# Two norms and a weight split inside the delta rule's last turn, with projection products behind it

## What is computed

```python
proj = _rmsnorm(x, mix_norm[i]) @ w_in[i]
q, k, v, z, beta_logit, alpha, hy_in = jnp.split(proj, IN_SPLITS, axis=-1)
o_dn = _deltanet_group(q, k, v, z, beta_logit, alpha, ...)   # 4 heads, both directions
o_hy = _hyena_group(hy_in, ...)                              # 512 channels
x = x + jnp.concatenate([o_dn, o_hy], axis=-1) @ w_out[i]
...
for o, gate in enumerate((x1, x2)):                          # in _hyena_group
    zz = gate * (_fft_conv(zz, kspec[:, o]) + skip[o] * zz)
return _rmsnorm(zz, norm_w).astype(u.dtype)
```

## Time and profile before

| what | us |
|---|---|
| median of 3 runs | 4145.75 |
| lowest, highest | 4143.84, 4146.04 |
| profiled execution | 4139.47 |
| its span, first to last instruction | 4137.7 |

### The profile page before, as it was taken

One profiled execution on the slowest core, in us unless ns is written; L12 is line 12 of the kernel. 1 busy time (PEld: TensorE's weight loads), 2 busy tenths in 40 slices (PEclk: granted clock), 3 DMA queues, 4 the chain that ended last, 5 costly groups with the idle time before them and its releaser, 6 DMA issues. The chain is left out here.

```text
span 4137.7 us, 46831 instructions
## 1 busy us (share of the span) xinstructions
PE 3937.5 (95%) x18392; PEld 3130.7 (76%) x18392; DVE 2264.6 (55%) x3096; ACT 1416.4 (34%) x1778; POOL 4.5 (0%) x13
## 2 busy tenths in 40 slices
PE   8999997989999999999798999979999999989998
PEld 6887853988888888784597888843677888877886
DVE  4335666555434434675665534577746773437763
ACT  4322421433322332341242332234333542334541
POOL 0000000000000000000000000000000000000000
PEclk9999998999999999999898999979999999999999
DMA  3223210002222322221001222300222222222222
GB/s 126 97 88 107 82 61 0 1 21 102 91 87 96 108 95 91 100 72 51 1 1 52 92 101 83 111 24 1 74 100 86 98 89 94 94 91 92 95 93 76
DMA packets 51509, 312.53 MB, mean 76 GB/s; under 512 B 6190, under 2 KB 6896, under 8 KB 23348
## 3 DMA queue, kind: packets, MB, share of 16 engines
q1 hardware_dynamic: 51380, 310.77, 21.8%
HBM read 308.65 MB, written 2.10 MB: 75 GB/s over the span
## 5 line engine op out<-in xcount | busy, mean ns | idle before, releaser
L145 PE MATMUL bank<-hidden_hi,w_hi 128*128 128x512 f32 x2688 | 1052.1, 391 | 23.9 <-DVE w_lo L180 13.1
L146 PE MATMUL bank<-hidden_lo,w_hi 128*128 128x512 f32 x2688 | 1048.3, 390 | 0.0
L147 PE MATMUL bank<-hidden_hi,w_lo 128*128 128x512 f32 x2688 | 1048.3, 390 | 0.0
L264 DVE TENSOR_TENSOR w_lo<-w_raw,w_hi 128x2048 fp32r<-128x2048 f32 (+1 forms) x279 | 575.0, 2061 | 395.8 <-ACT w_hi L259 383.7
L259 ACT ACTIVATE w_hi<-w_raw 128x2048 fp32r<-128x2048 f32 (+1 forms) x274 | 471.5, 1721 | 583.9 <-PE bank L147 538.2
L145 PEld LDWEIGHTS bank<-hidden_hi,w_hi 128*128 128x128 f32 x2688 | 505.9, 188 | 142.4 <-DVEq L251 14.9
L147 PEld LDWEIGHTS bank<-hidden_hi,w_lo 128*128 128x128 f32 x2688 | 506.0, 188 | 106.4
L146 PEld LDWEIGHTS bank<-hidden_lo,w_hi 128*128 128x128 f32 x2688 | 506.0, 188 | 104.4 <-issue 0.2
L145 PE MATMUL bank<-ffn_act_hi,w_hi 128*128 128x512 f32 x704 | 273.9, 389 | 0.0
L146 PE MATMUL bank<-ffn_act_lo,w_hi 128*128 128x512 f32 x704 | 273.9, 389 | 0.0
L147 PE MATMUL bank<-ffn_act_hi,w_lo 128*128 128x512 f32 x704 | 273.9, 389 | 0.0
(11 more groups left out here) (421 smaller groups left out, 5546.6 us busy)
## 6 DMA issues: line engine op xcount, KB each, us to landing
w_raw<-in_w_gu SPq DMA_DIRECT2D x132, 1024.0 KB, 4.8
w_raw<-in_w_down SPq DMA_DIRECT2D x96, 704.0 KB, 4.1
w_raw<-in_w_in SPq DMA_DIRECT2D x28, 1024.0 KB, 4.8
w_raw<-in_w_xattn SPq DMA_DIRECT2D x24, 1024.0 KB, 4.8
w_raw<-in_w_out SPq DMA_DIRECT2D x8, 1024.0 KB, 4.8
w_raw<-in_w_xattn_o SPq DMA_DIRECT2D x8, 1024.0 KB, 4.9
hyena_dft<-in_c_dft SPq DMA_DIRECT2D x6, 1024.0 KB, 10.0
w_raw<-in_w_qkv SPq DMA_DIRECT2D x6, 1024.0 KB, 5.0
```

Source lines behind the costliest of these rows:

```text
L145: nc.tensor.matmul(out, w_hi, x_hi, start=start, stop=False)
L146: nc.tensor.matmul(out, w_hi, x_lo, start=False, stop=False)
L147: return nc.tensor.matmul(out, w_lo, x_hi, start=False, stop=stop)
L264: nc.vector.tensor_tensor(self.lo[:, slot, 0:width], self.raw[:, slot, 0:width], self.hi[:, slot, 0:width].bitcast(F32), ALU.subtract)\
```

## The change

1. `hyena` ends after the last gating; its squares, root, scaling, transposes and splits move into `delta_rule`. The squares stand first in ScalarE's list there, the rest in the last turn, in the places where a piece of the next turn would stand.
2. The delta rule's two directions are added as they come out, in one tensor (`both`): turns 0 and 1 copy, turns 2 and 3 add. After turn 2 the two middle chunks are complete. They are normed and split during the last turn.
3. The last turn leaves out the new state (`k_end` rows, its products, its update).
4. The projection's first two tiles are loaded at the start of the last turn, and both slots are split in it: slot 0 after r1, slot 1 after r3.
5. Behind the last outputs, PE makes the projection's products over the branch's half (k = 4 to 7) in four groups of 12, with the last two chunks' column products and spreads between them. `delta_out` is gone as a stage. `pair_pe` then makes only k = 0 to 3 in its first turn. The delta stage still settles.
6. Some buffers lie elsewhere, and the lanes use other PSUM banks (2, 3, 0 and 4, 5, 1 instead of 0 to 2 and 3 to 5).

```diff
+    def out_products(self, pe, S, slot, j):
+        nc, m = self.nc, self.m
+        pe.wait_ge(S.sem("next_split"), slot + 1)
+        for k in range(KD // 2, KD):
+            c = slice((j * KD + k) * P, (j * KD + k + 1) * P)
+            product3(nc, m.bank[OUT_BANK + 2 * slot + j][:, :], m.w_hi[:, slot, c], m.w_lo[:, slot, c],
+                     m.o_hi[:, k, :], m.o_lo[:, k, :], start=(k == KD // 2), stop=False)
...
+        end = KD // 2 if first == "out" else KD
...
             last = product3(nc, m.bank[bank + 2 * slot + j][:, :], w_hi, w_lo, *x_tiles(k),
-                            start=(k == 0), stop=(k == KD - 1))
-            if k == KD - 1:
+                            start=(k == 0 and first != "out"), stop=(k == end - 1))
+            if k == end - 1:
...
+        hy_bank = (m.bank[7], m.bank[7], m.bank[7], m.bank[6])
...
+            for l in range(DIRS):
+                sp.wait_ge(sem("o_done", l), LAST)
+                sp.wait_ge(sem("x2_done", l), TT)
+                sp.wait_ge(sem("p1", l), TT)
+            then.load(sp, S)
```

PE's list in the turns (a second argument of `ahead` runs in the last turn only):

```diff
+            def mean_squares(n):
+                for l in range(DIRS):
+                    pe.wait_ge(sem("squared", l), n - TT + 3)
+                    for h in range(HEADS):
+                        at = (1 - l) * HEADS + h
+                        last = nc.tensor.matmul(stat_bank[n][:, at:at + 1], sqs[:, h, tokens(chunk(l, n))],
+                                                m.inv_d[:, 1:2], start=True, stop=True)
+                last.then_inc(S.sem("mean_square"), 1)
+            def inverse_spread(n, l):
+                pe.wait_ge(sem("diag", l), n - TT + 3)
+                nc.tensor.matmul(spread_bank[n][l][:, :], m.ones[:, :], diag[l][:, :, :], start=True, stop=True)\
+                    .then_inc(sem("inverse_spread", l), 1)
+            def hy_turned(c):
+                pe.wait_ge(S.sem("hy_scaled"), TT)
+                for t in range(TT):
+                    last = nc.tensor.transpose(hy_bank[c][:, t * P:(t + 1) * P], hy_rows[:, t, c * P:(c + 1) * P],
+                                               m.ident[:, :])
+                last.then_inc(S.sem("hy_turned"), 1)
...
+                def second_chunk():
+                    wait("weighed", 0, 0)
+                    inverse_spread(TT - 2, 1)
...
-                ahead(spread)
+                ahead(spread, lambda: mean_squares(TT - 2))
...
-                ahead(key_products)
+                ahead(key_products, lambda: hy_turned(0))
...
-                ahead(query_products)
+                ahead(query_products, lambda: inverse_spread(TT - 2, 0))
...
-                ahead(key_rows)
+                ahead(key_rows, lambda: hy_after(1, S.sem("hy_lo"), 1))
...
-                ahead(value_rows)
+                ahead(value_rows, second_chunk)
...
-                ahead(near_turned)
+                ahead(near_turned, lambda: hy_after(2, S.sem("hy_lo"), 2))
...
-                ahead(far_turned)
+                ahead(far_turned, lambda: hy_after(3, sem("weighed", 1), 1))
...
+            then.out_products(pe, S, 0, 0)
+            mean_squares(LAST)
+            then.out_products(pe, S, 0, 1)
+            then.out_products(pe, S, 1, 0)
+            for l in range(DIRS):
+                inverse_spread(LAST, l)
+            then.out_products(pe, S, 1, 1)
```

ScalarE's list:

```diff
+            hy_squares()
...
+                if n == LAST:
+                    squares(TT - 2)
+                    hy_root()
                 moves("x4_done", "x4_moved", n, lambda b: ((b.x4, 0), (b.x4_t, 1)))
-                ahead(grown)
+                ahead(grown, hy_scaled, lambda: root(TT - 2))
                 moves("x8_done", "x8_moved", n, lambda b: ((b.x8_t, 0),))
                 ahead(exponentials)
                 moves("p4_turned", "p4_moved", n, lambda b: ((b.x8_t, 0),))
+                if n == LAST:
+                    hy_upper(0)
                 moves("z_done", "z_moved", n, lambda b: ((b.x4, 0), (b.x4_t, 1)))
+                if n == LAST:
+                    hy_upper(1)
+                    then.split_act(act, S)
                 moves("z2_done", "z2_moved", n, lambda b: ((b.x2, 0), (b.x2_t, 1)))
-                ahead(near_moved)
+                ahead(near_moved, lambda: upper(TT - 2, 0), lambda: hy_upper(2))
                 moves("z4_done", "z4_moved", n, lambda b: ((b.x4_t, 0),))
-                ahead(far_moved)
+                ahead(far_moved, lambda: upper(TT - 2, 1), lambda: hy_upper(3), lambda: then.split_act(act, S, slot=1))
                 moves("v_done", "v_moved", n, lambda b: ((b.v_new, 2),))
...
+            squares(LAST)
+            root(LAST)
+            for l in range(DIRS):
+                upper(LAST, l)
```

VectorE's list:

```diff
-                ahead(masked_steps)
+                ahead(masked_steps, hy_inverse)
                 level(n, "p2", 1, ALU.add)
-                ahead(gaps)
+                ahead(gaps, lambda: scaled_square(TT - 2), lambda: gated(TT - 2, 0), lambda: gated(TT - 2, 1))
                 level(n, "p3", 0, ALU.add)
-                ahead(keys_beta)
+                ahead(keys_beta, lambda: inverse(TT - 2))
                 level(n, "p4", 1, ALU.add)
-                ahead(attention_part)
+                ahead(attention_part, lambda: weighed(TT - 2, 0), lambda: hy_lower(0), lambda: weighed(TT - 2, 1),
+                      lambda: hy_lower(1))
...
                 level(n, "r1", 0, ALU.subtract)
+                if n == LAST:
+                    then.split_dve(dve, S)
+                    lower(TT - 2, 0)
                 level(n, "r2", 1, ALU.add)
+                if n == LAST:
+                    hy_lower(2)
+                    lower(TT - 2, 1)
+                    hy_lower(3)
                 wanted(n)
                 level(n, "r3", 0, ALU.add)
...
+                if n == LAST:
+                    then.split_dve(dve, S, 1)
                 state(n)
...
+            for l in range(DIRS):
+                gated(LAST, l)
+            scaled_square(LAST)
+            inverse(LAST)
+            for l in range(DIRS):
+                weighed(LAST, l)
+            for l in range(DIRS):
+                lower(LAST, l)
```

More of the change, by code:

```diff
@@ L330, in residual_dve, with pair_pe @@
         square_dve(nc, m, steps, d, S.sem("squares"))
-def pair_pe(pe, nc, m, S, ring, i, base, x_tiles, first=False, free="pair_free", after=None, bank=0):
+def pair_pe(pe, nc, m, S, ring, i, base, x_tiles, first=None, free="pair_free", after=None, bank=0):
     for slot in range(2):
@@ L440, in _ @@
             h_tile = lambda k: (m.h_hi[:, k, :], m.h_lo[:, k, :])
-            pair_pe(pe, nc, m, S, ring, 0, 0, h_tile, first=True, free="banks_free")
+            pair_pe(pe, nc, m, S, ring, 0, 0, h_tile, first="pairs", free="banks_free")
             with pe.Fori(0, turns - 1) as i:
@@ L1411, in _, with pair @@
             values.pe = pe
-            def pair(turn, first=False):
+            def pair(turn, first=None):
                 def after(slot):
@@ L1861, in _ @@
             backward(1)
-            pe.wait_ge(S.sem("scaled"), TT)
-            for c in range(HYT):
-                for t in range(TT):
-                    last = nc.tensor.transpose(m.bank[4 + c][:, t * P:(t + 1) * P], z[:, t, c * P:(c + 1) * P],
-                                               m.ident[:, :])
-                last.then_inc(S.sem("turned"), 1)
         @S.block.scalar
@@ L2009, in delta_rule @@
[L2009 to L2030 removed]
+    return z
@@ L2031, in lane_buffers @@
             b.ahead = m.bank[6 + l]
-            return b
-        lanes = [lane_buffers(l) for l in range(DIRS)]
         def heads(bank):
@@ L2089, in key_rows @@
                 for l, b in enumerate(lanes):
-                    wait("attn", l, n)
-                    turn(b.ahead, part(1, l, n), sem("k_rows", l))
+                    if n < LAST:
+                        wait("attn", l, n)
+                        turn(b.ahead, part(1, l, n), sem("k_rows", l))
             def value_rows(n):
                 for l, b in enumerate(lanes):
-                    wait("k_end", l, n)
+                    if n < LAST:
+                        wait("k_end", l, n)
+                    else:
+                        wait("attn", l, n)
                     turn(b.ahead, part(2, l, n), sem("v_rows", l))
@@ L2345, in state @@
             def state(n):
+                if n < LAST:
+                    for l, b in enumerate(lanes):
+                        wait("o_done", l, n)
+                        for h in range(HEADS):
+                            last = nc.vector.scalar_tensor_tensor(
+                                b.state[:, h, :], b.state[:, h, :],
+                                gates.exp_last[:, chunk(l, n), 4 * l + h:4 * l + h + 1],
+                                b.bank[2][:, h * P:(h + 1) * P], op0=ALU.mult, op1=ALU.add)
+                        last.then_inc(sem("state", l), 1)
@@ L2346, in state @@
                 for l, b in enumerate(lanes):
                     wait("o_done", l, n)
```

(20 more changed lines are left out.)

286 lines of the change are left out of this document (156 added, 130 removed).

## The result

The median went from 4144.8 us (4143.4 to 4146.04, four runs) to **4075.46** (4072.07 to 4078.27, four runs): ratio 0.983 (0.9815 to 0.9849), 1.7% faster. The forecast was 4090 with 4077 to 4107. The profiled execution took 4072.73, of which the span is 4071.0; before it was 4139.47 and 4137.7. So the two profiled spans are 66.7 us apart, not 55.4.

The account below looks back on a forecast made before the run. PE was taken as busy 95% of the span, with latency-bound wait chains moved into a last turn where PE never rests. Per layer 12.7 + 0.9 - 9.5 + 24.6 - 1.0 = 27.7, twice 55.4, giving 4090 us, range 4077 to 4107.

Parts of the forecast that it names:

- branch end: Convolution branch's end: without its norm tail, the delta rule's first memset starts 12.67 us earlier; ScalarE's squares stay hidden.
- memset to last turn (turn 2's key rows): Delta rule, turn 2: eight transposes go where PE is full, 0.9 us less.
- last turn, with 1.0 for the clock: Delta rule's last turn: 9.5 us more (4.4 work, 5.1 waits), plus 1 us per layer for the clock.
- tail and projection: From the last outputs through the projection: 73.8 us becomes 49.2, gain 24.6 (bounds 21 and 27).
- The clock term: Last turn's new pauses of 2.6 and 2.2 us lower PE's clock: 1 us per layer, between 0 and 3.
- The table load: ScalarE's load before the root: 1.28 us without a drain; with one, PE would stand about 0.4 more per layer.
- Sum: Whole kernel: 27.7 us less per layer, 55.4 for two; profiled 4139.5 becomes 4084.1, plus 6.3 for the median, 4090.
- The last turn hides its work: Rival: the last turn costs only 4 to 6 us; time 4082, range 4076 to 4083; chance 0.12.
- Twice my waits: Rival: queue order makes the last turn cost 15 us and the clock 2; time 4103; chance 0.22.
- the projection runs dry: Rival: turn 1's weights or split come late, 3 us instead of 0.7; time 4095, within the forecast's range.
- slower than before: Rival: the last turn's pauses keep PE at 0.50 through it and the tail's products; time 4198; chance 0.03.
- It doesn't do what it says: Rival: tail products wait for the second split, needing 7 us of delay; chance 0.03 together with no change.

Follow-up runs that it names:

- v1_reorder: Changed kernel with PE's second transposed group moved behind z and VectorE's last three low parts behind the wanted values and r3: median 4076.0 us.
- u1_no_fill: Changed kernel with the projection products over the branch's half all placed behind the second chunks' steps instead of between them: median 4099.5 us.
- d3_before_delay8: Kernel before the change, with 8 idle small products added at the start of the self attention's stage: median 4138.4 us, ratio 0.998.
- v5_move_transposes: Changed kernel with only PE's second transposed group moved behind the products of z, VectorE's order untouched: median 4081.2 us.
- w2_after_busy: Changed kernel with 66 extra small products in PE's 17 us pause ahead of the self attention's transposes: median 4083.0 us, ratio 0.985.
- v3: v1_reorder with one extra 128 x 128 product in each of the first eleven steps of the self attention's heads: median 4084.3 us.
- v4: v1_reorder with two extra 128 x 128 products in each of the first eleven steps of the self attention's heads: median 4090.3 us.
- w3: Kernel before the change, with one extra 128 x 128 product in each of the first eleven steps of the heads: median 4147.2 us.

## Why the prediction was right in the mixers and wrong in the total

**The mixer, term by term** (layer 0, less per layer; the first column is the prediction's):

| term | predicted | measured | from |
|---|---|---|---|
| branch end | 12.7 | 12.45 | 14.78 to 2.33, last gating to memset |
| memset to last turn (turn 2's key rows) | 0.9 | 0.0 | 167.70 to 167.74 |
| last turn, with 1.0 for the clock | -10.5 | -10.3 | 35.2 to 45.5 |
| tail and projection | 24.6 | 24.4 | 73.8 to 49.3 |
| sum | 27.7 | 26.6 | |

- **Branch end: right.** The settled end cost VectorE 1.03 instead of 0.82 of waiting; that is the missing 0.2.
- **Turn 2: wrong, small.** Predicted 0.9, measured 0.4. The eight transposes went, but from the same product near its start to its end it takes 46.7 us before (822.6 to 869.3) and 46.4 after (809.1 to 855.5): the key rows were cover for ScalarE's move of x_t, and a pause of 0.49 stands there now (825.65). The 0.4 that was left went in the delta rule's first 22 us, whose clock was 0.73 instead of 0.77. "PE is full there" was no proof that each piece of PE work costs its time: I should have asked what the piece hides.
- **Last turn: right in place, and in size partly by luck.** Pauses of 2.56 and 1.79 for 2.6 and 2.2, at the entries named, and v1_reorder removes both by the two moves that the walk implies. The clock term was right in kind: a mean of 0.83 over 870 to 880 is 3.4 us at 0.50, behind the 2.56 pause, which costs some 1.7 us where I had allowed 1. In the other direction, the four waits that the walk lists (0.8, 0.4, 2.6, 2.2) make 6.0, while its sum has 5.1, and PE stood 4.4. A dearer clock and cheaper waits cancel.
- **Tail and projection: right** to 0.2, with PE busy 14.83 of the 16 us behind the outputs. u1_no_fill shows that the products are what hides the norm's chain.
- **The table load**: 1.28 in both kernels, with the root 0.01 and 0.02 behind it, so the walk without a drain held. The Trainium skill's "ScalarE: Activation LUTs" (section "What ACT_TABLE_LOAD costs") adds a drain; neither trace shows one.

The two mixers gave 53.4 where I had 55.4.

**The step that failed** is the one sentence under "Sum": "The profiled execution took 4139.5; less 55.4 it is 4084.1". It puts at nothing, without a reason, what the stages outside the mixers do, as if they stayed as they were in that execution. They gave 13.3 us, 13.0 of them in heads and rest. d3_before_delay8 has the same short heads and rest without the change; v1_reorder, v5_move_transposes, u1_no_fill and w2_after_busy have the change and give them back, all or most. So these 13 us go with how PE's clock happens to fall in unchanged stages, and no part of the mixers' sum stands for them. With 13.3 more and 2.0 less gained in the mixers, 4084.1 becomes 4072.8; measured were 4072.7. The second part of the same step, 6.3 added for the median over the profiled execution, was 2.7 in the kernel after; that is the other 3.6 of the 15 us. The 6.3 was no property to carry over: the profiled execution of before lies in its smaller heap of times, some 5 below the other.

**The rivals.** "The last turn hides its work" came nearer in the total (4082, range 4076 to 4083) and is wrong all the same: the turn took 10.3, not 4 to 6. A total near a rival's number doesn't make the rival right; only the stages do. "Twice my waits", "the projection runs dry" and "slower than before" are refuted by the turn's 45.5, the 0.68 of wait, and the clock of 0.96 and 1.00 in the turn and the tail. "It doesn't do what it says" is refuted by the same tail: no product there waits for the second split. The range failed because nothing in it stood for stages that the change doesn't touch. The profile of before did offer the row to bound it by: 20.8 us at clock 0.56 with PE busy 20.8.

**Still open** is what decides whether the spell begins. In the twelve traces whose transposes followed the full pause, the 48 transposes took 6.85 to 7.71 us in the nine with the spell and 7.88 to 7.95 in the three without. So it kept away where the clock rose a little *later* in them. That is a pattern, not a cause: I have no run that moves this alone, and delays of 1.8 and 3.6 us on v1_reorder didn't reach it. The short pause between transposes and score products, the other thing that stands ahead of the fall in every kernel, was never varied. No kernel tried beats after beyond doubt; one with v1_reorder's mixers and without the spell would, by my estimate from the table, take some 9.7 less, and none of these is it.

## What to carry to other kernels

Where engines take their lists in a fixed order, walk the lists entry by entry with measured durations: place and size of each foreseen pause came out to half a microsecond, and the walk also names the two moves that remove them. It missed one of 0.49, where taking work off PE laid bare a move that the work had covered. Then compare stage by stage, not by the total: here 9.7 us saved upstream came to nothing at the end, and eight idle products made the kernel before faster. Give the range a term for every stretch of the profile in which PE is busy and its clock is low, since such a stretch was there in one kernel and not in another that differs from it only upstream.

## What the runs showed of the hardware

- **PE can be fully busy and stay at half clock.** In the heads of the kernel before it was busy 20.8 of 20.8 us at 0.56, with 64-row score products and transposes; the clock rose only once the products with the values ran, and in v3, v4 and w3 extra products of 128 rows ahead of these didn't bring it back. In w2_after_busy it fell from 1.00 under the same work, behind pauses of no more than 2.3 and 1.5 us. The same instructions ran at 1.00 in after and d3_before_delay8. The Trainium skill's "TensorE: Matmul & The Clock Gate" (Part 1) has activity release the throttle; 20.8 busy us at half clock are against it, if products of any kind count. It also has the monitor of activity run freely, not from a kernel's start; a spell that comes and goes between kernels with the same instructions in that stage would fit that, but no run here shows it.
- **In the last turn a pause of 2.56 us ended the full clock, one of 1.79 did not.** Behind the first the clock was at 0.50 for 3.4 us of the ten from 870 to 880 (and again in layer 1, 2160 to 2170, also 0.83); behind the second it stayed at 1.00. In v1_reorder, without the first, 871 to 881 has 1.00.
- **A handful of idle products can speed a kernel up**: eight of them, 3.3 us of delay, in d3_before_delay8. The profiled execution took 12.3 us less than that of before, three of ten runs came out at 4127 to 4130 where before has none below 4136.4, and the median fell by 6.5. As a tuning means it is a lottery ticket: the same on v1_reorder brought nothing.
